# A kernel for a hybrid decoder layer: the second mixer's value sums in quarters of the array, and the key transpose moved to the front of a chunk's step

## What is computed

```python
s = jnp.einsum('bhclk,bhcsk->bhcls', q, k) * jnp.exp(log_d - m_row[..., None])
inter = jnp.exp(m_inter - m_row)
num = jnp.einsum('bhcls,bhcsv->bhclv', s, v) + inter[..., None] * jnp.einsum('bhcvk,bhclk->bhclv', c_prev, q)
den = jnp.sum(s, axis=-1) + inter * jnp.einsum('bhck,bhclk->bhcl', n_prev, q)
h = num / jnp.maximum(jnp.abs(den), jnp.exp(-m_row))[..., None]
```

## Time and profile before

| | |
|---|---|
| median of 3 runs | 1084.43 us |
| lowest and highest | 1084.13 and 1084.49 us |
| the profiled execution | 1084.31 us, its span 1082.6 us |
| PE busy | 1070.9 us, 99% of the span |
| VectorE, ScalarE, GpSimd busy | 728.0, 518.1 and 650.5 us |
| granted PE clock | 1.0, all through |

### The profile page before, as it was taken

One profiled execution on the slowest core, in us unless ns is written; L12 is line 12 of the kernel. 1 busy time (PEld: TensorE's weight loads), 2 busy tenths in 40 slices (PEclk: granted clock), 3 DMA queues, 4 the chain that ended last, 5 costly groups with the idle time before them and its releaser, 6 DMA issues.

```text
span 1082.6 us, 17830 instructions
## 1 busy us (share of the span) xinstructions
PE 1070.9 (99%) x6007; PEld 853.7 (79%) x6007; DVE 728.0 (67%) x1144; ACT 518.1 (48%) x1252; POOL 650.5 (60%) x437
## 2 busy tenths in 40 slices
PE   7999999999999999999999999999999999999997
PEld 6887777777777778888878888888778888888886
DVE  5965785775766858566856685669568332558897
ACT  7544755746646643454445454545564311131543
POOL 3577555556555459558965797569654444447441
PEclk9999999999999999999999999999999999999999
DMA  6225132132142141114311432132209524754324
GB/s 219 78 85 89 41 117 78 40 117 69 48 143 61 56 130 50 40 49 127 97 40 40 127 91 54 39 117 87 68 16 373 157 83 150 248 160 156 155 90 145
DMA packets 113849, 111.80 MB, mean 103 GB/s; under 512 B 7340, under 2 KB 96744, under 8 KB 112760
## 3 DMA queue, kind: packets, MB, share of 16 engines
q1 hardware_dynamic: 102648, 77.08, 23.8%
q10 hardware_dynamic: 11136, 33.88, 9.7%
HBM read 84.63 MB, written 26.31 MB: 102 GB/s over the span
## 4 chain that ended last, share of the span: by engine, by line
PE 97%; ACT 1%; DVE 1%; DMA 0%; issue 0%; DVEq 0%; ACTq 0%
PE ps L1047 63%; PE ps L1296 16%; PE ps L954 4%; PE ps L1137 2%; PE ps L1179 2%; PE ps L1186 2%; PE ps L1257 1%; PE ps L1181 1%; PE ps L1239 1%; PE ps L1254 1%; ACT ev L1393 1%; PE ps L1251 1%; PE ps L1267 1%; PE ps L1206 1%; PE ps L1244 1%; PE ps L996 1%
## 5 line engine op out<-in xcount | busy, mean ns | idle before, releaser
L804 POOL TENSOR_TENSOR ring_lo<-w,ring_hi 128x512 fp32r<-128x512 f32 x128 | 183.3, 1453 | 99.5 <-ACT ring_hi L1435 99.5
L804 POOL TENSOR_TENSOR ring_lo<-t,ring_hi 128x512 fp32r<-128x512 f32 x96 | 132.8, 1388 | 137.3 <-ACT ring_hi L1435 137.3
L1047 PE MATMUL ps<-s_hi,ring_hi 128*128 128x512 f32 x512 | 203.8, 398 | 0.0
L1047 PE MATMUL ps<-s_lo,ring_hi 128*128 128x512 f32 x512 | 200.3, 391 | 0.0
L1047 PE MATMUL ps<-s_hi,ring_lo 128*128 128x512 f32 x512 | 200.1, 391 | 0.0
L1047 PE MATMUL ps<-h_hi,ring_hi 128*128 128x512 f32 x384 | 151.7, 395 | 0.0
L1047 PE MATMUL ps<-h_lo,ring_hi 128*128 128x512 f32 x384 | 150.4, 392 | 0.0
L1047 PE MATMUL ps<-h_hi,ring_lo 128*128 128x512 f32 x384 | 149.9, 390 | 0.0
L1435 ACT ACTIVATE ring_hi<-w 128x512 fp32r<-128x512 f32 x128 | 77.4, 623 | 89.4 <-PE ps L1047 79.5
L1047 PEld LDWEIGHTS ps<-s_hi,ring_hi 128*128 128x128 f32 x512 | 96.2, 188 | 21.8 <-issue 3.3
L1047 PEld LDWEIGHTS ps<-s_hi,ring_lo 128*128 128x128 f32 x512 | 96.1, 188 | 20.1
(11 more groups left out here) (325 smaller groups left out, 2236.8 us busy)
## 6 DMA issues: line engine op xcount, KB each, us to landing
w<-in_w_in SPq DMA_DIRECT2D x128, 256.0 KB, 2.9
xs<-in_x SPq DMA_DIRECT2D x8, 512.0 KB, 7.3
ga_scratch<-ev ACTq DMA_DIRECT2D x4, 1024.0 KB, 4.0
u_scratch<-silu_z ACTq DMA_DIRECT2D x8, 512.0 KB, 2.8
c_rows<-c_scratch ACTq DMA_DIRECT2D x8, 512.0 KB, 6.9
gm_scratch<-ev ACTq DMA_DIRECT2D x4, 1024.0 KB, 5.1
w_raw<-in_w_branch_attn SPq DMA_DIRECT2D x8, 512.0 KB, 4.5
u_a_f<-u_scratch SPq DMA_DIRECT2D x4, 1024.0 KB, 9.1
```

What stands on the lines that cost most here:

```text
L804: return nc.gpsimd.tensor_tensor(flat(lo[:]), flat(raw_or_sum[:]), flat(hi[:]).bitcast(F32), ALU.subtract)
L1047: mm = nc.tensor.matmul(ps[:, bank, columns], w[:, k, :], h[:, k, columns], start=(m == 0), stop=(m == PRODUCT - 1))
```

## The change

1. The value sums of a chunk, for c from 1 to 7, are made in quarters of the array. The zero quarter (late keys, early queries) is left out of each head, so six quarter matmuls take the place of two full ones. They stand in two sets of three. The first set comes behind the queries times old state and ahead of the state's increment; the second comes behind the scores. In each set the matmuls of one half of the tokens write one head's bank and those of the other half the other head's, and in the second set it is the other way round. For late queries the second set adds to what the first has written, and so PE waits for first_sums, which the first set's last matmul signals, and passes again. In the last step (c = 8) the value sums are two full matmuls as before.
2. The value sums of head j go to bank X[2 + j] at columns 0 to 128, and inter_ps beside them in the same bank. VectorE reads the sums from two banks.
3. The transpose of the chunk's keys stands in front of the step, behind its waits. m_scores is signalled by the last scores matmul.
4. The semaphores s1_made and s324_made of the prologue become one, s_made.

```diff
         def inter_ps(rows, j):
-            return ps[rows, X[2 + j], 2 * (MV + 1) * (1 - j):2 * (MV + 1) * (1 - j) + MV + 1]
+            return ps[rows, X[2 + j], MV + 1:2 * (MV + 1)]
...
+                first, second, every = slice(0, 64), slice(64, 128), slice(0, P)
+
+                def values(m, j, tokens, out, start, stop):
+
+                    return nc.tensor.matmul(ps[out, X[2 + j], 0:MV + 1], dmat[tokens, j, out], v1[tokens, m, j, :],
+                                            start=start, stop=stop)
+
                 for c in range(NB + 1):
...
+                    if c < NB:
+                        tok = slice(c * P, (c + 1) * P)
+                        nc.tensor.transpose(ps[:, X[1], P:2 * P], mk_T[:, tok], ident[:])
                     pe.sem_inc(passed, 1)
...
+                        if c < NB:
+                            values(m, 0, first, first, True, True)
+                            values(m, 0, first, second, True, False)
+                            values(m, 1, second, second, True, False).then_inc(first_sums, 1)
                         if m < NB - 1:
...
-                                nc.tensor.matmul(ps[out, X[j], 0:P], mk_T[rows, keys], mq_T[rows, c * P:(c + 1) * P],
-                                                 start=True, stop=True)
-                        tok = slice(c * P, (c + 1) * P)
-                        nc.tensor.transpose(ps[:, X[1], P:2 * P], mk_T[:, tok], ident[:]).then_inc(m_scores, 1)
+                                mm = nc.tensor.matmul(ps[out, X[j], 0:P], mk_T[rows, keys], mq_T[rows, tok],
+                                                      start=True, stop=True)
+                        mm.then_inc(m_scores, 1)
+                    if 0 < c < NB:
+                        pe.wait_ge(first_sums, 7 * p + c)
+                        pe.sem_inc(passed, 1)
+                        values(m, 1, first, first, True, True)
+                        values(m, 1, first, second, False, True)
+                        mm = values(m, 0, second, second, False, True)
+                    if c == NB:
+                        for j in range(2):
+                            mm = values(m, j, every, every, True, True)
                     if c:
-                        for j in range(2):
-                            mm = nc.tensor.matmul(ps[:, X[2], j * (MV + 1):(j + 1) * (MV + 1)], dmat[:, j, :], v1[:, m, j, :],
-                                                  start=True, stop=True)
                         mm.then_inc(m_prod, 1)
...
-                    num = ps[:, X[2], 0:2 * (MV + 1)]
-                    h_c = v1[:, c].rearrange("p j n -> p (j n)")
+                    num = ps[:, X[2]:X[3] + 1, 0:MV + 1]
+                    h_c = v1[:, c]
...
-                        V.tensor_tensor(h_c, num, inter[:].rearrange("p j n -> p (j n)"), ALU.add).then_inc(m_state, 1)
+                        V.tensor_tensor(h_c, num, inter[:], ALU.add).then_inc(m_state, 1)
```

More of the change, by code:

```diff
@@ L338, in build @@
         hT_lo_ready = sem("hT_lo_ready")
-        s1_made = sem("s1_made")
-        s324_made = sem("s324_made")
+        s_made = sem("s_made")
         s_hi = sem("s_hi")
@@ L424, in build @@
         m_sT = sem("m_sT")
+        first_sums = sem("first_sums")
         m_prod = sem("m_prod")
@@ L1033, in turn_attention_v @@
                 mm.then_inc(v_turned, 1)
-            pe.wait_ge(s1_made, 1)
+            pe.wait_ge(s_made, 1)
             turn_attention_v(0)
@@ L1237, in mlstm_step @@
                                     rows, out = slice(64 * j, 64 * j + 64), slice(64 * half, 64 * half + 64)
-                                    tok = slice(m * P + 64 * half, m * P + 64 * half + 64)
-                                    nc.tensor.matmul(inter_ps(out, j), mq_T[rows, tok], state[rows, :], start=True, stop=True)
+                                    queries = slice(m * P + 64 * half, m * P + 64 * half + 64)
+                                    nc.tensor.matmul(inter_ps(out, j), mq_T[rows, queries], state[rows, :],
+                                                     start=True, stop=True)
[3 more added lines that the diff above has]
+                            values(m, 1, second, second, True, False).then_inc(first_sums, 1)
                         if m < NB - 1:
@@ L1494, in _ @@
             A(g_f[:, :], dense_ps(GATES)[32:40, :], ACT.Identity, bias=gate_bias[32:40, :]).then_inc(g_parts, 1)
-            act.wait_ge(s1_made, 1)
+            act.wait_ge(s_made, 1)
             A(s1[0][:], s1_f[:], ACT.Copy).then_inc(s_hi, 1)
-            act.wait_ge(s324_made, 1)
+            act.wait_ge(s_made, 2)
             A(s3[0][:], s3_f[:], ACT.Copy).then_inc(s_hi, 1)
-            act.wait_ge(s324_made, 2)
+            act.wait_ge(s_made, 3)
             A(s2[0][:], s2_f[:], ACT.Copy).then_inc(s_hi, 1)
@@ L2101, in _ @@
                                              f21[:, k - KH, :], ALU.mult, ALU.add)
-            ins.then_inc(s1_made, 1)
+            ins.then_inc(s_made, 1)
             V.tensor_tensor(f11[:], h11[0][:].bitcast(F32), h11[1][:].bitcast(F32), ALU.add)
@@ L2107, in _ @@
             dve.drain()
-            V.tensor_tensor(s3_f[:], f11[:], f21[:], ALU.subtract).then_inc(s324_made, 1)
-            V.tensor_tensor(s2_f[:], s1_f[:], f11[:], ALU.subtract).then_inc(s324_made, 1)
+            V.tensor_tensor(s3_f[:], f11[:], f21[:], ALU.subtract).then_inc(s_made, 1)
+            V.tensor_tensor(s2_f[:], s1_f[:], f11[:], ALU.subtract).then_inc(s_made, 1)
             V.tensor_tensor(f12[:], h12[0][:].bitcast(F32), h12[1][:].bitcast(F32), ALU.add)
@@ L2113, in _ @@
             dve.drain()
-            V.tensor_tensor(s4_sum[:], f12[:], s2_f[:], ALU.subtract).then_inc(s324_made, 1)
+            V.tensor_tensor(s4_sum[:], f12[:], s2_f[:], ALU.subtract).then_inc(s_made, 1)
             def low_part(s, full, n):
```

## The result

The changed kernel takes 1086.20 us, the median of 20 runs (1086.04 to 1086.58), against 1084.46 us for the kernel before, the median of 20 runs (1084.13 to 1084.96). The ratio is 1.0016, with a 95% interval from 1.0009 to 1.0023. So it is slower by 1.7 us, 0.16%, where +1.2 us and 1085.6 us were forecast, and inside the stated range of 1083.0 to 1089.0.

A forecast was written before the change was run, and what follows sets the result against it. TensorE's own stream, busy 99% of the span, was taken as the bound. 28 steps at +0.035 us (+1.0) and four first steps at +0.05 (+0.2) gave +1.2 us: 1085.6 us, eight-in-ten range 1083.0 to 1089.0.

The forecast's parts named there:

- The exit: Leaving quarters for a 512-column product or full-size values instead of a transpose: 0.20 against 0.15 us, 0.05 dearer per step.
- The values in quarters: Chunks 1 to 7: two sets of three take 0.44 against 0.45 us; the two left-out quarters save nothing.
- The transpose behind a product: Transpose at the step's front costs its own turn alone, 0.109 us; entry into quarters neither gains nor loses.
- The covered wait: TensorE's wait for first_sums before the second set: covered by state and scores with 0.10 us to spare, costing nothing.
- The step's sum: Per changed step: +0.05 exit, -0.01 values, -0.006 shorter sets, about +0.035 us, so 1.56 against 1.53.
- The products behind them pay nothing: Dense products (L1047) following a step's full-size value passes: claimed to carry no extra cost.
- The chunk period of 8.38 to 8.40 us: Sign of being right: the distance between chunk steps' starts grows from 8.35 us to this.
- the rival of the cheaper exit: Leaving quarters costs 0.15 us as today; sum -0.3 us, 1084.1; counted within the forecast's 0.66.
- The uncovered wait: Slower rival, between scores and second set, 28 times: 0.12 us exposed gives 1089.0, bound of 0.34 gives 1095.1; chance 0.22.
- The quarters' arithmetic (six in eight): Faster rival: issuing sets the price, so left-out quarters save 3.1 us, giving 1082.5; chance 0.12.
- VectorE's slack in the last pair: 1.65 us from k_w's end to the step needing it, covering all that could move on VectorE and ScalarE.
- one price for every border: Tiling-mode rule alone, all borders priced equally: only the values' 0.01 per step changes, some -0.3 us in all.

The follow-up runs named there:

- the kernel that uncovers it: Changed kernel with the first set of values moved behind the scores, directly ahead of the second set and its wait: 1097.03 us, ratio 1.0116 to the kernel before.
- the zero quarters: Changed kernel with the two left-out zero quarters put back, so each set is four quarters: 1086.37 us, 0.17 over the changed kernel.

## Why the prediction was right, and where it was short

Sums over the 32 changed steps are from the starts of all matmul records in the two traces: 1.37 us more in the steps, 0.63 us more in the products between them. Two differences outside these stretches stand beside them: 0.16 us more ahead of the first step, and 0.17 us less around the last pair's transposes of the result. Whether the change has a part in them was not tried; runs of one kernel differ by more, 1084.13 to 1084.96 us. Together they give 2.0, against spans that differ by 1.9 as printed and by 1.96 unrounded.

- **The exit** held. 0.05 dearer was forecast, and it is 0.19 to 0.20 into a product against 0.15 into a transpose. At c = 0 the steps grew by 0.047 each, with 0.05 forecast.
- **The values in quarters** held in mechanism: two sets at 0.22 for 0.45, and the left-out quarters save nothing. Putting them back costs 0.17 us in all, within the run's spread. In size they save less than the 0.016 us of the sum: at c = 2 to 7 the step with the transpose last is 0.005 shorter than before (1.979 against 1.984), and at c = 1 by 0.018.
- **The transpose behind a product** held: 0.23 behind it, and the entry into quarters as before. The moved transpose alone carries the whole loss.
- **The covered wait** held: no gap, no change without it, and 0.39 a step where nothing covers it, with 0.34 as forecast bound.
- **The step's sum** was 0.035. Measured, between the starts of the products around a step, are 0.041 to 0.045 at c = 2 and 4 to 7, 0.050 at c = 3 and 0.032 at c = 1. The kernel with only the transpose moved shows the parts: that move alone lengthens every step by 0.046 to 0.049, as the forecast exit has it, and the values then take off 0.004 to 0.006 (nothing at c = 3, 0.015 at c = 1), not the 0.016 of the sum.
- **"The products behind them pay nothing"** was the step that failed in size. This sentence was about the kernel before, and I carried it over to the new order without a term. It was wrong there already: from the second to the last of thirty products it is 6.367 us, 0.02 over the plain stream's 28 turns of 0.2267, and behind the changed step it is 6.387. That is 0.02 us more a step, 0.6 us in all. The products behind the attention's scores would have shown that such a cost exists, but not that it would grow: their second and twelfth starts lie 2.29 us apart (101.49 to 103.78, the row below), 0.02 over ten plain turns, no more than behind a step of the kernel before.

```profile
103.78 0.39 PE L1047 MATMUL ps<-s_hi,ring_lo 128*128 128x512 f32 x1
```

- **The number.** 1.2 us were forecast; the two medians differ by 1.74 and the two spans by 1.96. The steps' share, 1.37 with 1.2 forecast, was foreseen, and the products' 0.63 was not. The chunk period of 8.38 to 8.40 us missed for the same reason. One more slip is in the rival of the cheaper exit: with the prediction's own terms, an exit of 0.15 gives -0.4 us and not -0.3.
- **The rivals.** The uncovered wait did not come true, its price did in the kernel that uncovers it. The quarters' arithmetic (six in eight) is refuted by the scores' 192 columns in the earlier trace rows and by the zero quarters. VectorE's slack in the last pair is 1.75 us now, from k_w's end at 791.64 + 0.47 = 792.11 to the transpose at 793.86, against 1.65 in the earlier trace rows.

The rule from the Trainium skill's "TensorEngine Tiling (Array Packing)", Overview, Key Properties, that a change of tiling mode drains the engine, agrees with the traces here as far as each border costs time, 0.14 going in and 0.15 to 0.20 coming out, and a change of quarter does not. What decided was what the rule leaves open: the price depends on what comes behind the border. By one price for every border the change would have gained 0.3 us, and it lost 1.7.

## What stays open

Why the products behind a step are slower when the transpose does not stand between quarters and values. It happens with the transpose in front (values full or in quarters, with and without wait, in old and new banks) and with the transpose last. It is not the wait, the banks, more short matmuls, or when ScalarE and VectorE start. What all these kernels share is their order of work on PE; GpSimd's and the DMA's traffic were not tried as a cause, nor was any part of PE by itself. The traces give one clue. The distances of the starts behind a step, from the second product on, mostly run into one and the same tail. Behind c = 3 of the second pair they are, in ns, 231, 230, 236, 229, 232, 231, then 227 in the kernel before, and 240, 235, 233, 236, 224, 231, 236, 228, 233, 231, then 227 in the changed one. The order ahead decides how early in this tail the stream begins; what makes the tail is open.

## What to carry to other kernels

Where small matmuls on quarters are laid into a stream of full-size ones, count the borders and look at what stands behind each. Here the cheapest thing to stand behind quarters was a short full-size operation with a short weight load (the transpose, an exit of 0.15 us against 0.19 to 0.20), and moving it to the other end lost that. Leaving out one quarter of four saved nothing here, since the other three still took every pass; count passes per quarter, not matmuls. A wait of PE on itself was free where the work between signal and wait outlasted the release, here about 0.5 us from the start of the signalling set, and cost 0.39 us where nothing lay between.

## What the runs showed of the hardware

- The weight load behind the last quarter pass starts 0.20 us after that pass's start, before a transpose (440.84 to 441.04) as before a product (441.65 to 441.85); the transpose's turn follows 0.06 later, the product's 0.10.
- TensorE waiting on its own matmul: the first load behind the wait starts 0.53 us after the first start of the set whose last matmul signals (441.88 to 442.41).
- Products of 512 columns behind an interruption of the dense stream start mostly 0.23 to 0.24 us apart for up to ten turns before they settle at 0.227. How long this lasts differs with the order ahead of them (0.02 us in sum in the kernel before, 0.04 in the changed one), and doubling the scores did not lengthen it.
- A set of three quarters and a set of four both take 0.22 us for two passes of 129 columns, and a free quarter goes ahead with later work (L1259 at 440.87 beside L1227) without the others gaining by it.
